# A hybrid decoder step: RMS norms by chunk made from 128x3 values, x turned where it is used, w_ada split in two

## The chip, the cores and the metric

The kernel runs on one core of one Trainium2 chip. The core has a matrix engine (PE, which loads stationary weights with LDWEIGHTS, in the profile PEld, and streams a moving operand past them into PSUM), VectorE (DVE), ScalarE (ACT), GpSimd (POOL) and SyncE (SP, which here only starts DMAs). The metric is device time in microseconds for one launch; lower is better.

## The reference, cut to what matters

One layer: attention and pooling branches, then two sandwiched residual steps and an MLP, for 1024 prompt tokens and 8 sample tokens. Shift, scale and gate vectors come from a conditioning vector c through `w_ada`.

```python
def rms_norm(x, g):
    y = x32 * lax.rsqrt(jnp.mean(x32 * x32, axis=-1, keepdims=True) + EPS)
    return (y * g.astype(jnp.float32)).astype(x.dtype)
def adaln(c, w_ada, b_ada):                    # w_ada is 1024 x 6144
    m = jnp.einsum('nd,de->ne', jax.nn.silu(c), w_ada) + b_ada
    ...
    m = jnp.einsum('ntd,de->nte', m, w_o)
    x = x + gate1 * rms_norm(m, g_post_mix)
    h = rms_norm(x, g_pre_mlp) * (1.0 + scale2) + shift2
    f = einsum(square(relu(einsum(h, w_ff1))), w_ff2)
    x = x + gate2 * rms_norm(f, g_post_mlp)
```

## The kernel before

All activations lie feature by token: a tile is [128 features, KD = 8 feature blocks, T = 1032 tokens]. Products are made in fp32r, a fast form of fp32 with fewer bits: each operand is split into a high part (ACT copies it, `hi`) and a rest (POOL or DVE subtracts, `lo`), and hi·hi + hi·lo + lo·hi are added in PSUM. Semaphores order everything; every engine runs its own list in order.

**Stage A (rest of the projection into the layer, with the last two thirds of w_ada).** Fifteen units u: `g.multiply` (72 products 344 wide), then on PE `turn_ada(u-1)` and `condition(u)`. `condition` multiplies 256 columns of `w_ada` with the 9 conditioning columns `cT`, in plain fp32, straight from the DMA's buffer `wa` (two slots). ACT and POOL only split the projection's weights (`cut_hi`, `cut_lo`), in a loop. A sixteenth `condition` follows the last unit.

**Stage B (chunks).** The tokens are cut into three chunks of 384, 384 and 264 (256 prompt, 8 sample). PE runs 24 products with w_o (`wo(n)`, n = 0..23, eight output blocks for each chunk, each 24 matmuls) and then 12 with the first blocks of w_ff1 (`up_chunk(n)`, n = 24..35), through four PSUM banks. For each chunk there are two norms: of w_o's result (`sum_mo`, then `make_x1` adds it to x) and of the new x (`sum_x1`, then `make_h2`). ACT squares, POOL adds the squares up over the eight feature blocks, PE multiplies the 128x384 sums with a matrix of ones, so that every partition holds every token's sum, and `stats` makes 1/rms on DVE over 128x384 values. POOL multiplies half of the blocks with it (`scale`). x comes in token by feature early, is turned by PE (`turn_x`) between `wo(2)` and `wo(7)` and copied to `xT` by DVE (`take_x`).

**Stage C (main MLP).** 52 weight tiles of 72 products, one after the other. **Stage D (end).** The last w_ff2 products chunk by chunk (`end(n)`, 24 of them), the third norm for each chunk (`sum_y`, `make_y`), the result turned back (`turn_y`) and written out.

## Time and profile before

| | us |
|---|---|
| timed runs | 2067.61, 2073.70, 2076.02 (median 2073.70) |
| the profiled execution | 2078.76, with a span of 2077.0 from first to last instruction |
| stage A, 71 to 309 | 238 |
| attention and pooling, 309 to 1128 | 819 |
| stage B, 1128 to 1362 | 234 |
| stage C, 1362 to 1956 | 594 |
| stage D, 1956 to 2077 | 121 |

The profiled execution is one run with the hardware profiler on; its own time lies 5.06 us above the median of the timed ones. A table by stage shows the share of each stretch in which an engine had work, and the granted clock of PE in that stretch (1.00 is 2.4 GHz, 0.50 is 1.2 GHz).

### The profile page before, as it was taken

The numbers are of one execution on the slowest core, as the hardware profiler recorded it, in microseconds if no ns is written. First come the engines' busy times: TensorE is split into PE (matmuls) and PEld (weight loads), VectorE is DVE, ScalarE is ACT, GpSimd is POOL, SyncE is SP. The second block draws the span as 40 slices with busy tenths as digits, with TensorE's granted clock in tenths as the row PEclk, the third lists the DMA queues.
The fourth block names the chain that finished last, engine by engine and source line by source line (L and its number), as shares of the span: only waits on it lengthen the run. The fifth ranks groups of instructions, "written<-read, shape, count | busy, mean of one in ns | idle before, by whom it ended". The sixth has DMA issues, their size and how long they took to land. (4 is left out here: it accounts for less than half of the span.)

```text
span 2077.0 us, 26057 instructions
## 1 busy us (share of the span) xinstructions
PE 1806.8 (87%) x10834; PEld 1640.5 (79%) x10834; DVE 759.6 (37%) x1381; ACT 555.9 (27%) x1042; POOL 606.7 (29%) x457
## 2 busy tenths in 40 slices
PE   6899995678889888896799786599999999999996
PEld 2788874467777776774699776599999999999996
DVE  2311114244456555663334468721121112111246
ACT  3200001024445544552224123321022012102312
POOL 1211101014445543441024147322112111211332
PEclk9899997988989998998699998799999999999998
DMA  8343325301110100002254002121111111111412
GB/s 265 82 119 95 98 66 162 88 24 42 45 35 28 35 24 21 21 28 79 84 168 137 32 31 71 32 61 41 51 46 47 48 45 51 42 51 41 132 47 67
DMA packets 210486, 139.24 MB, mean 67 GB/s; under 512 B 53317, under 2 KB 206065, under 8 KB 210329
## 3 DMA queue, kind: packets, MB, share of 16 engines
q1 hardware_dynamic: 195611, 124.14, 20.9%
q10 hardware_dynamic: 14758, 13.44, 2.0%
q8 instruction: 86, 1.41, 0.3%
q14 instruction: 31, 0.25, 0.0%
HBM read 117.95 MB, written 21.92 MB: 67 GB/s over the span
## 5 line engine op out<-in xcount | busy, mean ns | idle before, releaser
L1257 POOL TENSOR_SCALAR prob<-prob,share 128x16 f32<-128x16 f32 (+8 forms) x180 | 198.7, 1122 | 290.0 <-DVE share L1296 290.0
L1971 POOL TENSOR_TENSOR ff_lo<-ff_raw,ff_hi 128x1024 fp32r<-128x1024 f32 x56 | 137.0, 2449 | 481.3 <-ACT ff_hi L1792 481.3
L1087 PE MATMUL gate_ps<-h_hi,gate_w_hi 128*128 128x344 f32 x384 | 144.6, 377 | 17.7 <-ACT gate_sum L1214 10.6
L172 POOL TENSOR_TENSOR w_lo<-w_raw,w_hi 128x512 fp32r<-128x512 f32 (+1 forms) x31 | 55.7, 1801 | 331.3 <-ACT w_hi L168 241.2
L2110 PE MATMUL ff_acc<-h_hi,ff_hi 128*128 128x344 f32 x672 | 142.7, 321 | 0.6 <-DVE relu_c L2257 0.6
L2110 PE MATMUL ff_acc<-h_lo,ff_hi 128*128 128x344 f32 x672 | 142.7, 321 | 0.0
L2110 PE MATMUL ff_acc<-h_hi,ff_lo 128*128 128x344 f32 x672 | 141.9, 320 | 0.0
L1306 DVE TENSOR_TENSOR p_lo<-pT,p_hi 128x512 fp32r<-128x512 f32 (+1 forms) x148 | 101.8, 688 | 106.9 <-ACT p_hi L1196 106.3
L1185 ACT ACTIVATE prob<-scores,bias 128x640 f32<-128x640 f32 (+7 forms) x192 | 105.8, 556 | 96.8 <-DVE bias L1282 58.0
L1196 ACT ACTIVATE p_hi<-pT 128x512 fp32r<-128x512 f32 (+1 forms) x148 | 88.2, 596 | 159.2 <-PE pT L1141 158.4
L1087 PE MATMUL gate_ps<-h_lo,gate_w_hi 128*128 128x344 f32 x384 | 128.6, 335 | 0.0
L1087 PE MATMUL gate_ps<-h_hi,gate_w_lo 128*128 128x344 f32 x384 | 128.5, 335 | 0.0
L1141 PE MATMUL pT<-ident,prob 128*128 128x128 f32 (+1 forms) x592 | 96.9, 289 | 34.1 <-POOL prob L1257 34.1
L2110 PE MATMUL ff_acc<-f_hi,ff_hi 128*128 128x344 f32 x576 | 122.5, 321 | 1.8 <-issue 1.8
L2110 PE MATMUL ff_acc<-f_lo,ff_hi 128*128 128x344 f32 x576 | 122.3, 321 | 0.0
L2110 PE MATMUL ff_acc<-f_hi,ff_lo 128*128 128x344 f32 x576 | 121.7, 320 | 0.0
L1792 ACT ACTIVATE ff_hi<-ff_raw 128x1024 fp32r<-128x1024 f32 x56 | 58.7, 1051 | 217.8 <-DMA ff_raw<-in_w_ff_dram 217.8
L2110 PEld LDWEIGHTS ff_acc<-h_lo,ff_hi 128*128 128x128 f32 x672 | 113.8, 189 | 0.0
L2110 PEld LDWEIGHTS ff_acc<-h_hi,ff_hi 128*128 128x128 f32 x672 | 113.1, 188 | 0.8 <-issue 0.8
L2110 PEld LDWEIGHTS ff_acc<-h_hi,ff_lo 128*128 128x128 f32 x672 | 112.0, 188 | 0.0
L1141 PEld LDWEIGHTS pT<-ident,prob 128*128 128x128 f32 (+1 forms) x592 | 69.3, 142 | 52.7 <-POOL prob L1257 37.3
L2339 DVE TENSOR_SCALAR relu<-ff_acc 128x1032 f32<-128x1032 f32 x28 | 34.5, 1233 | 200.1 <-PE ff_acc L2110 200.1
(368 smaller groups left out, 4087.1 us busy)
## 6 DMA issues: line engine op xcount, KB each, us to landing
ff_raw<-in_w_ff_dram SPq DMA_DIRECT2D x56, 512.0 KB, 4.0
wa_rest<-in_w_ada_dram SPq DMA_DIRECT2D x16, 1024.0 KB, 5.3
gate_spill<-gate_sum SPq DMA_DIRECT2D x48, 172.0 KB, 1.9
gates<-gate_spill SPq DMA_DIRECT2D x16, 516.0 KB, 4.8
wa<-in_w_ada_dram SPq DMA_DIRECT2D x8, 1024.0 KB, 9.8
gate_w_raw<-in_w_in_dram SPq DMA_DIRECT2D x16, 512.0 KB, 4.1
w_raw<-in_w_in_dram SPq DMA_DIRECT2D x30, 256.0 KB, 6.3
xt<-in_x_prompt_dram ACTq DMA_DIRECT2D x4, 1024.0 KB, 9.3
```

The costliest lines, as they stand in the source:

```text
L172: pool.tensor_tensor(self.w.lo[:, s, 0:k], self.w.raw[:, s, 0:k], self.w.hi[:, s, 0:k].bitcast(F32), ALU.subtract).then_inc(self.lo_ready, 1)
L1087: last = pe.matmul(gps[:, 0:CH], a[:, u % 2, k], h[:, k, c * CH:(c + 1) * CH], start=(k == 0 and n == 0), stop=(k == KD - 1 and n == 2))
L1141: last = pe.transpose(pT[t % RING][0:m, g * P:(g + 1) * P], prob[:, g, c:c + m], ident[:])
L1185: last = act.activation(prob[:, k, to:to + m], ps[:, c0:c0 + m], ACT.Exp, scale=SCALE, bias=bias[:, par, k, which:which + 1], accum_out=to ...
L1196: act.activation(p_hi[0:m, t % RING], pT[t % RING][0:m, :], ACT.Copy).then_inc(phi_ready, 1)
L1257: last = pool.tensor_scalar(y, y, share[:, n // 2 % 2, g, which:which + 1], None, ALU.mult)
L1306: dve.tensor_tensor(p_lo[0:m, t % RING], pT[t % RING][0:m, :], p_hi[0:m, t % RING].bitcast(F32), ALU.subtract)\
L1792: act.activation(hi, raw, ACT.Copy).then_inc(wfhi_ready, 1)
L1971: pool.tensor_tensor(lo, raw, hi.bitcast(F32), ALU.subtract).then_inc(wflo_ready, 1)
L2110: last = pe.matmul(accs[s][:, c, 0:CH], w[:, z % SLOTS, k], x[:, k, c * CH:(c + 1) * CH], start=(k == 0 and n == 0), stop=(k == KD - 1 and ...
L2339: dve.tensor_scalar(by_chunk(relu[:]), out(m % 2), 0.0, None, ALU.max).then_inc(ff_taken[m % 2], 1)
```

## The change

**w_ada.** `wa` is split like every other weight: ACT copies it to `wa_hi` (one buffer), POOL subtracts into `wa_lo` (in the place of `wa`). c is split too (`c_st`, 9 high and 9 rest columns). `condition` is now two fp32r products for each feature block, 18 and 9 columns wide; the two halves of the 18 rows are added when the rows are turned (a product with `fold`). The ACT and POOL loops are written out, a `cut_ada` after every `cut`.

**Norms.** `add_up` makes the sum for each token with the squares as the stationary operand and one column of ones: 128x1 for each block of 128 tokens, 128x3 in all. `stats` works on 128x3. `spread_out` multiplies 1/rms, broadcast along the free axis, with the identity, and so spreads it over all partitions in PSUM, where DVE reads it. `norm_bank` has two banks. POOL's `scale` and `end_scale` are gone: DVE multiplies all blocks. In `make_h2` DVE only multiplies; the scale and shift is an activation on ACT (`h2_shift`).

**x.** The three x blocks of a chunk are loaded later, into parts of `xT` that are free by then. PE turns them two feature blocks at a time between or in the middle (`halfway`) of products, and `make_x1` reads the turned block from PSUM. The copies to `xT` are gone; `turn_x` waits for `x1_ready`, since there are two PSUM tiles for it.

The norms at the end (`sum_y`, `stats`, `make_y`) are changed in the same way, and `turn_y` pairs are moved one or two products earlier in the list.

```diff
             def condition(pe, c):
-                pe.wait_ge(wa_loaded[c % 2], 16 * (c // 2 + 1))
+                pe.wait_ge(walo_ready, c + 1)
                 if c:
                     pe.wait_ge(arow_ready, c)
+                else:
+                    pe.wait_ge(cst_ready, 1)
                 for k in range(KD):
-                    last = pe.matmul(adaP[:], cT[:, k], wa[:, c % 2, k], start=(k == 0), stop=(k == KD - 1))
+                    pe.matmul(adaP[:], c_st[:, k], wa_hi[:, k], start=(k == 0), stop=False, skip_group_check=True)
+                    last = pe.matmul(adaP[0:1 + NS], c_st[:, k, 0:1 + NS], wa_lo[:, c % 2, k], start=False, stop=(k == KD - 1),
+                                     skip_group_check=True)
                 last.then_inc(ada_done, 1)
...
-                    last = pe.transpose(adaT[:, n], arow[:, c % 2, n * P:(n + 1) * P], ident[0:1 + NS, 0:1 + NS])
+                    last = pe.matmul(adaT[:, n], arow[:, c % 2, n * P:(n + 1) * P], fold[:], start=True, stop=True)
...
+            def cut_ada_hi(act, c):
+                act.wait_ge(wa_loaded[c % 2], 16 * (c // 2 + 1))
+                if c:
+                    act.wait_ge(ada_done, c)
+                act.activation(wa_hi[:], wa[:, c % 2], ACT.Copy).then_inc(wahi_ready, 1)
+            def cut_ada_lo(pool, c):
+                pool.wait_ge(wahi_ready, c + 1)
+                pool.tensor_tensor(wa_lo[:, c % 2], wa[:, c % 2], wa_hi[:].bitcast(F32), ALU.subtract).then_inc(walo_ready, 1)
...
                 def _(act):
-                    with act.Fori(1, NU // 2) as j:
-                        g.cut_hi(act, j, 0)
-                        g.cut_hi(act, j, 1)
-                    g.cut_hi(act, NU // 2, 0)
+                    act.activation(c_st[:, :, 0:1 + NS], cT[:], ACT.Copy).then_inc(chi_ready, 1)
+                    cut_ada_hi(act, 0)
+                    for u in range(NU):
+                        if u + 2 < NU:
+                            g.cut_hi(act, u // 2 + 1, u % 2)
...
+        def x_block(c, b, k):
+            if c == 2:
+                return xlast[:, b, k]
+            if c == 1 and b == 2:
+                return xthird[:, k]
+            at_column = CUT[c + 1][0] + b * P
+            return xT[:, k, at_column:at_column + P]
...
+                    def load_x(dst, b, c):
+                        sp.dma_start(dst, xb[:, b]).then_inc(x_loaded[c], 16)
+                    sp.wait_ge(mlo_ready[1], KD)
+                    for b in range(3):
+                        load_x(xT[:, :, CUT[1][0] + b * P:CUT[1][0] + (b + 1) * P], b, 0)
+                    sp.wait_ge(mlo_ready[2], KD)
+                    for b in range(2):
+                        load_x(xT[:, :, CUT[2][0] + b * P:CUT[2][0] + (b + 1) * P], 3 + b, 1)
...
+                    sp.wait_ge(x1_ready, 2 * KD)
+                    for b in range(2):
+                        load_x(xlast[:, b], 6 + b, 2)
+                    sp.dma_start(xlast[0:NS, 2], x_sample[:, 0, :].rearrange("n (k j) -> n k j", k=KD)).then_inc(x_loaded[2], 16)
                     spill(1)
...
+                    def h2_shift(c, k):
+                        t = h2[:, k, CUT[c][0]:CUT[c][0] + PROMPT[c]]
+                        act.wait_ge(h2t_ready, c * KD + k + 1)
+                        act.activation(t, t, ACT.Identity, scale=sc2[:, k, 0:1], bias=ada[:, 3 * KD + k, 0:1]).then_inc(h2_ready, 1)
                     def h2_cut(c, k0, k1):
+                        h2_shift(c, k0)
                         for k in range(k0, k1):
+                            if k + 1 < k1:
+                                h2_shift(c, k + 1)
                             act.wait_ge(h2_ready, c * KD + k + 1)
...
-                    def scale(c):
-                        pool.wait_ge(rstd_ready, 2 * c + 1)
-                        for k in range(1, KD, 2):
-                            pool.tensor_tensor(part(term[:, k], c), mo[c][:, k, 0:WIDTH[c]], rstd[:, 0:WIDTH[c]], ALU.mult)\
-                                .then_inc(scaled, 1)
...
+                    def turn_x(c, k0, k1):
+                        for k in range(k0, k1):
+                            e = c * KD + k
+                            if k == 0:
+                                pe.wait_ge(x_loaded[c], 48)
+                            if e >= 2:
+                                pe.wait_ge(x1_ready, e - 1)
+                            for b in range(3):
+                                m = NS if c == 2 and b == 2 else P
+                                last = pe.transpose(tp[e % 2][:, b * P:b * P + m], x_block(c, b, k)[0:m], ident[0:m, 0:m])
+                            last.then_inc(xT_done, 1)
...
+                    def add_up(count, c, squares):
+                        for b, m in tokens_of(c):
+                            last = pe.matmul(norm_bank[count % 2][0:m, CW + b:CW + b + 1], squares[:, b * P:b * P + m], ones[:, 0:1],
+                                             start=True, stop=True)
+                        last.then_inc(summed, 1)
+                    def spread_out(count, c, r):
+                        pe.wait_ge(rs_ready, count)
+                        for b, m in tokens_of(c):
+                            last = pe.matmul(norm_bank[count % 2][:, b * P:b * P + m], r[0:m, b:b + 1].broadcast_to([m, P]), ident[0:m, 0:m],
+                                             start=True, stop=True)
+                        last.then_inc(spread, 1)
...
                     def sum_mo(c):
                         pe.wait_ge(sq_added, (KD - 1) * (c + 1))
                         if c:
-                            pe.wait_ge(mean_ready, 2 * c)
-                        pe.matmul(nps[:, 0:WIDTH[c]], ones[:], sqsum[:, 0:WIDTH[c]], start=True, stop=True).then_inc(summed, 1)
+                            pe.wait_ge(x1_ready, KD * c)
+                        add_up(2 * c + 1, c, sqsum)
...
+                    def halfway(c, k0, k1):
+                        return lambda k: turn_x(c, k0, k1) if k == KD // 2 else None
...
                     for n in range(KD):
                         wo(n, before=(lambda k: pe.wait_ge(mlo_ready[0], k + 1)) if n == 0 else None)
-                        if n >= 2:
-                            for e in range(4 * (n - 2), 4 * (n - 1)):
-                                turn_x(e)
                     wo(8)
-                    pe.wait_ge(x_loaded[3], 16)
-                    pe.wait_ge(xT_taken, 3 * KD - 1)
-                    for k in range(KD):
-                        last = pe.transpose(tp[0][:, k * NS:(k + 1) * NS], xblk2[0:NS, 0, k * P:(k + 1) * P], ident[0:NS, 0:NS])
-                    last.then_inc(xT_done, 1)
                     sum_mo(0)
-                    for n in range(9, 13):
-                        wo(n)
+                    wo(9)
+                    spread_out(1, 0, rs)
+                    turn_x(0, 0, 2)
+                    wo(10, halfway(0, 2, 4))
+                    turn_x(0, 4, 6)
+                    wo(11, halfway(0, 6, 8))
+                    wo(12)
+                    wo(13)
                     sum_x1(0)
-                    for n in range(13, 17):
-                        wo(n)
...
+                    def stats(count, r, v, t):
                         dve.wait_ge(summed, count)
-                        dve.tensor_scalar(v[:, 0:w], nps[:, 0:w], 1.0 / D, EPS, ALU.mult, ALU.add).then_inc(mean_ready, 1)
+                        dve.tensor_scalar(v[:], norm_bank[count % 2][:, CW:CW + 3], 1.0 / D, EPS, ALU.mult, ALU.add).then_inc(mean_ready, 1)
                         dve.wait_ge(root_ready, count)
-                        chain.then_wait(dve.reciprocal(r[:, 0:w], r[:, 0:w]))
-                        chain.then_wait(dve.scalar_tensor_tensor(t[:, 0:w], r[:, 0:w], -0.5, r[:, 0:w], ALU.mult, ALU.mult))
-                        chain.then_wait(dve.tensor_tensor(t[:, 0:w], t[:, 0:w], v[:, 0:w], ALU.mult))
-                        dve.scalar_tensor_tensor(r[:, 0:w], t[:, 0:w], 1.5, r[:, 0:w], ALU.add, ALU.mult).then_inc(rstd_ready, 1)
-                        dve.wait_ge(rstd_ready, count)
-                    def residual(x, t, gate, c):
+                        chain.then_wait(dve.reciprocal(r[:], r[:]))
+                        chain.then_wait(dve.scalar_tensor_tensor(t[:], r[:], -0.5, r[:], ALU.mult, ALU.mult))
+                        chain.then_wait(dve.tensor_tensor(t[:], t[:], v[:], ALU.mult))
+                        dve.scalar_tensor_tensor(r[:], t[:], 1.5, r[:], ALU.add, ALU.mult).then_inc(rs_ready, 1)
...
                     def make_x1(c, k0, k1):
+                        w = WIDTH[c]
+                        dve.wait_ge(spread, 2 * c + 1)
                         for k in range(k0, k1):
+                            e = c * KD + k
                             t = part(term[:, k], c)
-                            if k % 2:
-                                dve.wait_ge(scaled, 4 * c + k // 2 + 1)
-                            else:
-                                chain.then_wait(dve.tensor_tensor(t, mo[c][:, k, 0:WIDTH[c]], rstd[:, 0:WIDTH[c]], ALU.mult))
-                            residual(part(xT[:, k], c), t, gt1[:, k], c).then_inc(x1_ready, 1)
+                            chain.then_wait(dve.tensor_tensor(t, mo[c][:, k, 0:w], norm_bank[1][:, 0:w], ALU.mult))
+                            dve.wait_ge(xT_done, e + 1)
+                            residual(part(xT[:, k], c), t, gt1[:, k], tp[e % 2], c).then_inc(x1_ready, 1)
...
                     def make_h2(c, k0, k1):
                         p, w = PROMPT[c], WIDTH[c]
+                        dve.wait_ge(spread, 2 * c + 2)
                         for k in range(k0, k1):
                             t = part(h2[:, k], c)
-                            chain.then_wait(dve.tensor_tensor(t, part(xT[:, k], c), rstd[:, 0:w], ALU.mult))
                             if p < w:
+                                chain.then_wait(dve.tensor_tensor(t[:, p:w], xT[:, k, TP:T], norm_bank[0][:, p:w], ALU.mult))
                                 chain.then_wait(dve.tensor_tensor(t[:, p:w], t[:, p:w], sc2[:, k, 1:], ALU.mult))
                                 dve.tensor_tensor(t[:, p:w], t[:, p:w], ada[:, 3 * KD + k, 1:], ALU.add)
-                            dve.tensor_scalar(t[:, 0:p], t[:, 0:p], sc2[:, k, 0:1], ada[:, 3 * KD + k, 0:1], ALU.mult, ALU.add)\
-                               .then_inc(h2_ready, 1)
+                            dve.tensor_tensor(t[:, 0:p], xT[:, k, CUT[c][0]:CUT[c][0] + p], norm_bank[0][:, 0:p], ALU.mult).then_inc(h2t_ready, 1)
...```

What stands on DVE from the last `wo` copy before the first norm to the first x1 blocks, before (`rstd`, `mean` and `ntmp` are the norm's 128x384 tiles, `term` the scaled result of w_o):

```order
L2201 COPY mo_10169<-ff_acc 128x384
L2280 COPY xT<-x_tp 128x8x8
L2212 TENSOR_SCALAR mean<-ff_acc 128x384
L2214 RECIPROCAL rstd<-rstd 128x384
L2215 SCALAR_TENSOR_TENSOR ntmp<-rstd 128x384
L2216 TENSOR_TENSOR ntmp<-ntmp,mean 128x384
L2217 SCALAR_TENSOR_TENSOR rstd<-ntmp,rstd 128x384
L2201 COPY mo_10169<-ff_acc 128x384 x2
L2235 TENSOR_TENSOR term<-mo_10166,rstd 128x384
L2226 SCALAR_TENSOR_TENSOR xT<-term,gt_60,xT 128x384 x2
```

The same place on DVE after (`mv`, `rs`, `nt` are the 128x3 tiles, `ff_acc` in the products is 1/rms in PSUM):

```order
L2310 COPY mo_10405<-ff_acc 128x384
L2315 TENSOR_SCALAR mv<-ff_acc 128x3
L2317 RECIPROCAL rs<-rs 128x3
L2318 SCALAR_TENSOR_TENSOR nt<-rs 128x3
L2319 TENSOR_TENSOR nt<-nt,mv 128x3
L2320 SCALAR_TENSOR_TENSOR rs<-nt,rs 128x3
L2310 COPY mo_10405<-ff_acc 128x384
L2337 TENSOR_TENSOR term<-mo_10402,ff_acc 128x384
L2328 SCALAR_TENSOR_TENSOR xT<-term,gt_60,x_tp 128x384
```

The five steps of the norm are three values wide, one copy stands between them and the first x1 block instead of two, and x is read from `x_tp`.

On POOL from the adds of w_o's first chunk to those of the second, before (`sqsum` takes the squares of w_o's result, `h` those of x1, `h_lo` is the rest of h2):

```order
L1937 TENSOR_TENSOR sqsum<-sqsum,sq 128x384 x7
L1949 TENSOR_TENSOR term<-mo_10166,rstd 128x384 x4
L1937 TENSOR_TENSOR sqsum<-sqsum,sq 128x384 x3
L1958 TENSOR_TENSOR h_10158<-h_10158 128x384 x7
L1937 TENSOR_TENSOR sqsum<-sqsum,sq 128x384 x4
L1964 TENSOR_TENSOR h_lo<-h_10158,h_hi 128x384 x8
L1949 TENSOR_TENSOR term<-mo_10169,rstd 128x384 x4
```

The same on POOL after:

```order
L2007 TENSOR_TENSOR sqsum<-sqsum,sq 128x384 x8
L2021 TENSOR_TENSOR h_10394<-h_10394 128x384 x3
L2007 TENSOR_TENSOR sqsum<-sqsum,sq 128x384
L2021 TENSOR_TENSOR h_10394<-h_10394 128x384 x4
L2007 TENSOR_TENSOR sqsum<-sqsum,sq 128x384 x3
L2027 TENSOR_TENSOR h_lo<-h_10394,h_hi 128x384 x4
L2007 TENSOR_TENSOR sqsum<-sqsum,sq 128x384
L2027 TENSOR_TENSOR h_lo<-h_10394,h_hi 128x384 x4
L2007 TENSOR_TENSOR sqsum<-sqsum,sq 128x384
```

The products with 1/rms are gone, and the last two adds of the second chunk's squares (n = 14 and 15), which stood ahead of all `h_lo` of the first chunk, now stand between and behind them.

## Rows read from the trace of the kernel before

**Rows 1.** The page's first part: engines' busy time, share of span, instructions.

```profile
PE 1806.8 (87%) x10834; PEld 1640.5 (79%) x10834; DVE 759.6 (37%) x1381; ACT 555.9 (27%) x1042; POOL 606.7 (29%) x457
```

**Rows 2.** Busy time by stage: stretch, length, engines, PE clock, DMA share, GB/s.

```profile
71.00:309.00 238.00, 235.91 (x1368) 197.43 (x1368) 27.34 (x54) 13.73 (x13) 30.46 (x14) 0.99 0.38 100
1128.00:1362.00 234.00, 170.88 (x949) 164.01 (x950) 155.73 (x241) 68.20 (x135) 106.88 (x89) 0.85 0.17 55
1362.00:1956.00 594.00, 592.16 (x3748) 591.62 (x3749) 98.41 (x81) 110.19 (x108) 128.52 (x53) 1.00 0.16 46
```

**Rows 3.** Timeline of one unit of stage A: start, length, engine, work, [wait].

```profile
161.59 1.06 ACT L168 ACTIVATE w_hi<-w_raw 128x1024 fp32r<-128x1024 f32 x1 [14.32 <-PE in_acc L202]
161.64 3.62 PE L516 MATMUL ada_rest<-wa_rest,cT 128*9 128x256 f32 x16
162.73 2.34 POOL L172 TENSOR_TENSOR w_lo<-w_raw,w_hi 128x1024 fp32r<-128x1024 f32 x1 [13.04 <-ACT w_hi L168]
165.19 0.74 PE L202 MATMUL in_acc<-h_hi,w_hi 128*128 128x344 f32 x3
...
176.96 3.41 PE L516 MATMUL ada_rest<-wa_rest,cT 128*9 128x256 f32 x15
```

**Rows 4.** Timeline of PE, the end of stage A.

```profile
299.52 3.62 PE L516 MATMUL ada_rest<-wa_rest,cT 128*9 128x256 f32 x16
...
303.87 3.62 PE L516 MATMUL ada_rest<-wa_rest,cT 128*9 128x256 f32 x16
```

**Rows 5.** Timeline of PE in stage B: turning x, and waits.

```profile
1147.40 1.33 PE L2031 MATMUL x_tp<-ident,x_three 128*128 128x128 f32 x6 [4.56 <-DVE xT L2207]
...
1179.75 0.82 PE L2031 MATMUL x_tp<-ident,x_three 128*128 128x128 f32 x6
...
1221.27 1.65 PE L2067 MATMUL ff_acc<-h,ones 128*128 128x384 f32 x2 [9.49 <-POOL h L1958]
...
1346.68 0.59 PE L2018 MATMUL ff_acc<-h_hi,wo_hi 128*128 128x264 f32 x1 [7.69 <-POOL h_lo L1964]
```

**Rows 6.** The chain that ended last, PE's pieces: start, us, what.

```profile
1128.02 9.97 PE ff_acc L2018 x48
...
1189.31 4.21 PE ff_acc L2018 x24
...
1346.68 14.60 PE ff_acc L2018 x96
...
2027.49 2.90 PE ff_acc L2018 x24
```

**Rows 7.** Timeline of DVE in stage B: a reciprocal, and h2.

```profile
1197.44 2.55 DVE L2214 RECIPROCAL rstd<-rstd 128x384 f32<-128x384 f32 x1 [1.90 <-ACT rstd L1771]
...
1238.67 1.37 DVE L2243 TENSOR_TENSOR h<-xT,rstd 128x384 f32<-128x384 f32 x1
```

**Rows 8.** Two lines on DVE: count, ns min/median/max, first and last start, forms.

```profile
L2226 DVE SCALAR_TENSOR_TENSOR xT<-term,gt,xT x24: 473/798/1368, 1205.3 to 1320.8; 128x384 f32<-128x384 f32 x16, 128x256 f32<-128x256 f32 x8
...
L2364 DVE TENSOR_TENSOR fT<-ff_acc,fT x24: 415/558/559, 1961.2 to 2053.7; 128x384 f32<-128x384 f32 x16, 128x264 f32<-128x264 f32 x8
```

**Rows 9.** Timelines of ACT and POOL, runs of operations without a wait between.

```profile
1126.76 3.42 ACT L1751 ACTIVATE m_hi<-mT 128x384 fp32r<-128x384 f32 x8 [9.03 <-PEq L1525]
...
1201.85 4.26 POOL L1949 TENSOR_TENSOR term<-mo,rstd 128x384 f32<-128x384 f32 x4 [12.91 <-DVE rstd L2217]
```

**Rows 10.** Groups by line and form on DVE: count, busy us, mean ns.

```profile
L2207 DVE COPY xT<-x_tp 128x384 f32<-128x384 f32 x16 | 8.2, 551 | 0.9 <-PE x_tp L2031 0.9
L1295 DVE RECIPROCAL share<-share 128x4 f32<-128x4 f32 x32 | 5.7, 179 | 1.1
```

**Rows 11.** The chain in stage D: sum of the last chunk, and its first product.

```profile
2055.48 0.73 PE ff_acc L2147 x2
...
2060.39 0.44 DVE yterm L2375
```

**Rows 12.** Timeline of PE in stage D: turning the second chunk's result.

```profile
2050.11 0.66 PE L2158 MATMUL x_tp<-ident,yterm 128*128 128x128 f32 x4 [1.24 <-DVE yterm L2226]
```

More of the change, by code:

```diff
@@ new lines, in _ @@
+                    cut_wo_hi(act, 4)
+                    for k in range(4):
+                        m_cut(1, k)
+                    cut_wo_hi(act, 5)
+                    for k in range(4, KD):
+                        m_cut(1, k)
+                    square(0)
+                    cut_wo_hi(act, 6)
+                    for k in range(4):
+                        m_cut(2, k)
+                    square(1)
+                    cut_wo_hi(act, 7)
+                    for k in range(4, KD):
+                        m_cut(2, k)
@@ L1825, in _ @@
+                    for n in range(2, 9):
+                        square(n)
+                    root(1)
                     square(9)
+                    x1_squares(0, 0, 4)
                     square(10)
-                    x1_squares(0, 0, 4)
+                    x1_squares(0, 4, 8)
                     square(11)
-                    x1_squares(0, 4, 8)
                     square(12)
+                    root(2)
                     square(13)
-                    root(2, 0)
+                    h2_cut(0, 0, 4)
@@ L2053, in up_chunk, with tokens_of @@
                         _, hi, lo = weights(t)
-                        product(bank[n % 4], hi, lo, h2_hi, h2_lo, c).then_inc(prod_done, 1)
+                        product(bank[n % 4], hi, lo, h2_hi, h2_lo, c, before).then_inc(prod_done, 1)
+                    def tokens_of(c):
+                        return [(b, NS if c == 2 and b == 2 else P) for b in range(3)]
+                    def add_up(count, c, squares):
[9 more added lines that the diff above has]
+                        last.then_inc(spread, 1)
                     def sum_mo(c):
@@ L2089, in _ @@
+                    spread_out(3, 1, rs)
+                    turn_x(1, 0, 2)
+                    wo(18)
+                    turn_x(1, 2, 4)
+                    wo(19)
+                    turn_x(1, 4, 6)
+                    wo(20)
+                    turn_x(1, 6, 8)
+                    wo(21)
+                    wo(22)
                     sum_x1(1)
-                    for n in range(22, 24):
-                        wo(n)
+                    wo(23)
+                    spread_out(4, 1, rs)
@@ L2092, in _ @@
                     up_chunk(24)
                     sum_mo(2)
-                    for n in range(25, 29):
-                        up_chunk(n)
+                    up_chunk(25)
+                    spread_out(5, 2, rs)
+                    turn_x(2, 0, 2)
+                    up_chunk(26, halfway(2, 2, 4))
+                    turn_x(2, 4, 6)
+                    up_chunk(27, halfway(2, 6, 8))
+                    up_chunk(28)
                     sum_x1(2)
-                    for n in range(29, 36):
+                    up_chunk(29)
@@ L2098, in _ @@
+                    spread_out(6, 2, rs)
+                    for n in range(30, 36):
                         up_chunk(n)
@@ L2280, in _ @@
-                    dve.tensor_copy(xT[:, :, TP:T], tp[0][:, 0:KD * NS].rearrange("p (k n) -> p k n", k=KD)).then_inc(xT_taken, 1)
-                    stats(1, WIDTH[0], rstd, mean, ntmp)
+                    for k in range(4):
+                        m_rest(1, k)
+                    collect(0)
+                    for k in range(4, KD):
+                        m_rest(1, k)
+                    collect(1)
+                    for k in range(4):
+                        m_rest(2, k)
+                    collect(2)
```

302 lines of the change are left out of this document (148 added, 154 removed).

## The prediction

> **What bounds the kernel now.** I read the page's first part, then a table by stage, then timelines of the stages that the change touches, then the chain. PE is busy 1806.8 us, 87% of the span [rows 1]: this is a kernel of matrix products, and a change is worth what it takes off PE's work or off PE's waits. The table by stage [rows 2] says which of the two, where. Stage A: PE busy 235.9 of 238 us at clock 0.99, so only less work on PE helps. Stage B: 170.9 of 234 at clock 0.85; 63 us are waits, and part of the busy time is slow. Stage C: 592.2 of 594 at 1.00, and the change doesn't touch it. So I build stages A, B and D from their rows, against the profiled execution (2078.76 us, span 2077.0), which is 5.06 above the median of 2073.70.
>
> **Stage A, w_ada.** A condition holds PE from 161.64 to 165.19, 3.55 us; the next starts at 176.96, so a unit takes 15.32 and 11.77 lie between conditions [rows 3]. After, it is 16 fp32r products 256 wide. Nearest row: 24 fp32r products 264 wide in 2.90 [rows 6], 0.121 each, so 0.117 at 256 and 1.88 for 16; the fold costs 0.14 more (one transpose more at 0.82/6 [rows 5]). Saved: 3.55 - 2.02 = 1.53, in 15 units 23.0.
> That row is 0.117 for a product. The Trainium skill ("TensorE: Matmul & The Clock Gate", section "Back-to-back issue gap") gives 262 cycles at a moving size of 256; by it 16 products would take about 1.75 (an estimate), and the units 2 us more would be saved. I go by the row.
> Cover: wa has to be cut first, and `wa_hi` is one buffer, so the cut starts when the last condition ends. ACT 128x2048 costs twice 1.06, POOL twice 2.34 [rows 3], with hand-offs 0.2: 2.1 + 4.7 + 0.2 = 7.0, against 11.8 of the multiply: hidden, 4.8 to spare. Behind these two steps `cut_hi` and `cut_lo` for two units on are queued; they have a unit's time. The load of wa into the freed slot has a whole period. If this cover failed, the units would be longer by what is missing, bounded by the gain (0).
> The sixteenth condition has no multiply ahead: PE starts it at 303.87, 0.7 after the end of the one at 299.52 [rows 4]. After, it waits for the 7.0: +6.3, less a gain of 0.6 (its own products are shorter, but come after a wait): +5.7. Stage A: -23.0 + 5.7 = **-17.3**, bounds -23 and 0.
>
> **Stage B, PE's work.** It lasts from 1128.02 to stage C's first tile at 1361.9, 233.9 us. Its products in full flow: 4.21 for 384 columns, 2.90 for 264 [rows 6], so 24 x 4.21 + 12 x 2.90 = 135.8. The first two take 9.97, not 8.42 [rows 6]: +1.55. Turning x: 64 transposes at 0.137 [rows 5] and 8 small ones, 9.4. Norms: six sums and six spreads of three small products; none is in the trace. The nearest row is 0.73 for two records of a sum [rows 11], the bounds are 0.5 (three transposes, with the wait for the weights) and 1.3 (under the 1.65 at [rows 5]); I take 0.75, 9.0 in all, bounds 6 to 15.6. Together 155.8.
>
> **What goes.** Turning waits for DVE's copies 16 times, 4.56 us the first time [rows 5]; the copies (16 of 0.551 and the smaller ones [rows 10]) go, and x is turned after the sum, when the bank is free. The 384-wide reciprocal of 2.55 [rows 7] becomes a step on 128x3, nearest row 0.179 on 128x4 [rows 10]; so does each other step. The norm's chain after the sum is then five such steps, a root and a spread, 1.5 to 3 us, and lies under `wo(9)` (4.2) or `up_chunk`s (2.9). POOL's products, four at 4.26 us a chunk [rows 9], go. `make_x1`'s sum takes 0.473 to 1.368 with both operands in SBUF, while a DVE operation that reads PSUM never exceeds 0.559 [rows 8]: two engines that read SBUF seem to get into each other's way (inferred; the spread is the fact), and the new operands are in PSUM. So the 9.49 wait before the first chunk's second sum [rows 5] should go, and `wo(0)` to `wo(8)` run without a gap.
> The Trainium skill ("VectorE: DVE Perf Modes", "Rules for kernel authors") advises to copy from PSUM to SBUF first where many operations read it. By that rule 24 copies more, about 13 us of DVE, would pay for themselves; by [rows 8] an operation from PSUM costs 0.56 at 384 columns, as much as a copy, so I don't count them.
>
> **What is late next.** Three waits of PE remain or are new.
> (1) `sum_mo(1)`. From the second spread PE has `wo(15)` and `wo(16)`, 7.1 us. In the new order POOL does eight `h_lo` and two adds first, 10 x 1.07 (4.26/4 [rows 9]) = 10.7, and starts 1.8 later (one DVE product, two ACT steps of 0.5). 12.5 - 7.1: 5.4, less 0.2 for what else PE does there: 5.2.
> (2) Chunk 2's turns. Two tiles hold the turned x, so each pair of turns waits until DVE has done with the pair before. A block there is two operations of 0.42 [rows 8] and two on 8 columns of 0.18 [rows 10], 1.2, a pair 2.4, and DVE takes a product's result between pairs, 0.55; PE has half of an `up_chunk` of chunk 0 and a pair of turns beside it, 2.1 + 0.27. Lost: 0.5 three times, 1.5. In chunk 0 a pair takes 2 x 1.07 (0.56 and 0.5) and every second one 0.55 more: about covered; in chunk 1 whole products stand between.
> (3) `up_chunk(32)`. From the last spread PE has 8.4 (two `up_chunk`s and turning's rest). DVE makes eight blocks of h2 at 1.2 (one 0.42 product, three 8-column ones at 0.18 and 0.2 for their hand-offs; bounds 0.9 and 1.5), 9.6, and the relu of `up_chunk(30)`, which stands behind them in DVE's list, 0.5; behind that wait on ACT `hidden_chunk(30)` and the cuts of h2, eight at 0.43 (3.42/8 [rows 9]) with the 264-wide less, 4.1 with the first's hand-off, then POOL 0.8: 15.0. The wait is 6.6, much like today's 7.69 there [rows 5].
> Together 13.3, between 0 and 25. After a wait PE is slow: the last four products take 14.60 instead of 11.60 after 7.69 of waiting [rows 5, 6], 3.0; I count it for (3) and two thirds of it for (1): 5. x itself is not late, I expect: chunk 0's loads start when the low part of the second chunk's input is made, some six products (25 us) before the turns; the last chunk's stand behind four loads of weights in SP's list and have, by my estimate, 5 us to spare, the smallest margin; if that is gone, PE waits there for what is missing.
> Stage B: 155.8 + 13.3 + 5 = 174.1, so **-59.8**; bounds -78 (none of the waits) and -40 (15.6 for the norms and nearly twice the waits).
>
> **Stage D.** From the end of the last sum (2055.48 + 0.73) to the first product with 1/rms (2060.39) are 4.2 us [rows 11]; after, five steps of 0.18, a root, hand-offs and a spread, 2.2: -2.0. Two earlier spreads cost 1.4 (two of 0.7), and PE's wait for `make_y(1)`, 1.24 [rows 12], goes, since the turns move behind another product. Behind the sum DVE takes POOL's four products, 4 x 0.46 (0.415 to 0.558 [rows 8]) = 1.9; POOL no longer runs beside it, for which I take back 1.3, one and a half times the 0.9 between a delayed operation and a free one (1.368 - 0.473 [rows 8]). Together **-1.2**, bounds -4 and +3. Stage C: 0.
>
> **Sum.** -17.3 - 59.8 - 1.2 = -78.3. The profiled execution goes from 2078.8 to 2000.5, the median from 2073.7 to **1995**.
>
> **Rivals.**
> (a) The waits don't come: POOL and ACT are ahead, DVE's operations take 0.47, as the fastest do [rows 8]. Then 13.3 + 5 go too: 1977. For: [rows 8] shows the fast case. Against: (1) and (3) are sums of many operations, in an order that is fixed.
> (b) DVE sets stage B: its x1 and h2 operations keep the longest time that they show today, 1.37 [rows 7, 8]. A pair in chunk 0 is then 2 x (0.56 + 1.37) = 3.9 against 2.4, 1.5 lost three times, 4.5, and 1.0 for the result taken between; in chunk 2, with 0.91 at 256 columns, 3.4 and 0.3 against 2.4, 1.3 three times, 3.9, of which 1.5 is counted; h2 in (3) is later by 8 x 0.5 = 4; and PE is slow after each of six more waits by some 0.8 (5 us for the two large ones above), 5. Together 4.5 + 1.0 + 2.4 + 4 + 5 = 17, 2012. For: DVE now does all that POOL did. Against: those that took so long had POOL beside them and read SBUF alone.
> (c) The cut of w_ada is not hidden, or its products are no faster: stage A gains nothing, 2013. For: one buffer, so ACT, POOL and PE go in turn. Against: 4.8 us to spare.
> (d) Slower than before. PE is at clock 0.85 in stage B and 1.00 in stage C [rows 2]; if the turns, spreads and waits in the middle of products keep it at 1.2 GHz there, 135.8 us of products take twice that: 1995 + 136 = 2131. It decides from 78.3/135.8, 58% of them at the lower level. Against: today's stage has longer waits and products still take 4.21 [rows 6].
> (e) The change does not do what it says: stage A gains nothing, as in (c), and in stage B each wait that goes comes back as another, so that PE waits the 63 us of today and its products are slow behind them as today. Only stage D's 1.2 stay: 2072.5. Against: the longest of today's waits hang on operations that are no longer there.
>
> **How the numbers follow.** Forecast 0.48 (its own range 1985 to 2006), (a) 0.17, (b) 0.20, (c) 0.10, (d) 0.03, (e) 0.02. The range must reach into (a), to 1972, since the norms may cost 3 us less too and stage A may reach its -23; upwards past (b) and (c), to 2020. A measurement of this kernel can tell about 0.5% (10 us) from no change: all of the forecast, (a), (b) and (c) are faster by more, 0.95; (e) is the same, 0.02; (d) is slower, 0.03.
>
> **What would show it.** Right: in stage A conditions of 1.9 us in periods of 13.8, no wait for POOL in the units, one of 7 before the last condition. In stage B `wo(0)` to `wo(8)` without a gap; waits of about 5 before `sum_mo(1)` and 6.6 before `up_chunk(32)`; the two DVE lines of x1 near 0.56 with none at 1.37; spreads of 0.75. Stage C as long as before at 1.00. Wrong: periods near 15.3; PE waiting for DVE before turns (b); a clock in stage B under 0.85 (d); a last-chunk wait for x's load, which I took to have a margin of 5.

## The result

The changed kernel took 2004.0 us (median of 2003.52, 2003.8, 2004.2 and 2008.4), the kernel before, timed beside it, 2074.86: a ratio of 0.9668 with a 95% interval of 0.9638 to 0.9697. The forecast was 1995, with a range of 1972 to 2020. The profiled execution took 2003.8 us, with a span of 2002.0.

The page's first part and its row of TensorE's clock, after:

```profile
PE 1776.5 (89%) x10956; PEld 1641.2 (82%) x10956; DVE 692.9 (35%) x1366; ACT 595.6 (30%) x1083; POOL 648.1 (32%) x449
...
PEclk9899987879989998999689999999999999999998
```

[rows 1] had PE at 1806.8. So TensorE's work fell by 30 us, while the time fell by 71: more than half of the gain is waiting that is gone. The table by stage says where, as in [rows 2] (stretch, length, busy time of PE, PEld, DVE, ACT and POOL, PE clock, DMA share, GB/s). The cuts are now at PE's own instructions: first condition, start of the last product of the last one, first `wo` product, first tile of the main MLP, first product of the end. After:

```profile
84.40:290.10 205.70, 199.68 (x1325) 189.75 (x1323) 26.26 (x49) 42.59 (x28) 100.01 (x28) 0.98 0.40 103
290.10:1106.44 816.34, 656.57 (x3903) 561.33 (x3901) 393.14 (x864) 308.00 (x697) 274.64 (x227) 0.89 0.21 62
1106.44:1282.26 175.82, 162.62 (x1008) 159.19 (x1009) 97.32 (x212) 77.46 (x159) 86.65 (x77) 0.94 0.24 73
1282.26:1879.91 597.65, 591.94 (x3744) 591.14 (x3745) 98.07 (x80) 110.33 (x108) 128.60 (x53) 1.00 0.16 46
1879.91:2002.00 122.09, 107.24 (x686) 104.10 (x684) 47.30 (x107) 28.47 (x51) 34.00 (x27) 0.92 0.31 92
```

The same cuts before gave 222.10, 820.92, 233.87, 593.48 and 121.63. Set against the forecast:

| stretch | before | after | change | forecast |
|---|---|---|---|---|
| stage A, w_ada | 222.1 | 205.7 | -16.4 | -17.3 |
| attention, pooling | 820.9 | 816.3 | -4.6 | 0 |
| stage B, chunks | 233.9 | 175.8 | -58.1 | -59.8 |
| stage C, main MLP | 593.5 | 597.7 | +4.2 | 0 |
| stage D, end | 121.6 | 122.1 | +0.5 | -1.2 |

In stage B PE waits 175.8 - 162.6 = 13.2 us; it waited 63.1. The list of PE's waits there (who waited, for whom: us in total, times, the longest), after:

```profile
PE ff_acc L2078 <- POOL h_lo L2027: 6.0, 1, 6.0
PE ff_acc L2124 <- POOL sqsum L2007: 5.1, 1, 5.1
PE ff_acc L2078 <- DVE m_lo L2303: 4.3, 1, 4.3
PE ff_acc L2132 <- DVE rs L2320: 1.5, 2, 1.0
PE ff_acc L2211 <- DVE relu_c L2360: 0.6, 1, 0.6
```

The 4.3 lie ahead of the stage's first product, as before. The same list of the kernel before began with what has gone:

```profile
PE ff_acc L2067 <- POOL h L1958: 34.3, 3, 12.8
PE x_tp L2031 <- DVE xT L2207: 12.4, 6, 4.6
PE ff_acc L2018 <- POOL h_lo L1964: 11.1, 2, 7.7
```

The 34.3 were three waits for the second norm of each chunk (POOL's adds, behind x1, behind POOL's own products), the 12.4 those for the copies of x.

### The profile page after: what moved, and what is told of

It is laid out like the page before. It is cut to its first block and busy times, and to the rows that moved or that the text cites. A ratio compares the mean times of both kernels' runs of the same rounds, so it can differ in the third digit from the quotient of the medians.

```text
span 2002.0 us, 26313 instructions
## 1 busy us (share of the span) xinstructions
PE 1776.5 (89%) x10956; PEld 1641.2 (82%) x10956; DVE 692.9 (35%) x1366; ACT 595.6 (30%) x1083; POOL 648.1 (32%) x449
## 5 line engine op out<-in xcount | busy, mean ns | idle before, releaser
L1119 PE MATMUL gate_ps<-h_hi,gate_w_hi 128*128 128x344 f32 x384 | 143.0, 372 | 18.3 <-ACT gate_sum L1246 11.1
L2211 PE MATMUL ff_acc<-h_hi,ff_hi 128*128 128x344 f32 x672 | 142.7, 321 | 0.6 <-DVE relu_c L2360 0.6
L2211 PE MATMUL ff_acc<-h_lo,ff_hi 128*128 128x344 f32 x672 | 142.6, 321 | 0.0
L2211 PE MATMUL ff_acc<-h_hi,ff_lo 128*128 128x344 f32 x672 | 141.9, 320 | 0.0
L172 POOL TENSOR_TENSOR w_lo<-w_raw,w_hi 128x512 fp32r<-128x512 f32 (+1 forms) x31 | 56.4, 1821 | 233.7 <-ACT w_hi L168 143.5
L2211 PE MATMUL ff_acc<-f_lo,ff_hi 128*128 128x344 f32 x576 | 122.3, 321 | 3.7 <-issue 3.7
L2211 PE MATMUL ff_acc<-f_hi,ff_hi 128*128 128x344 f32 x576 | 122.4, 321 | 2.0 <-issue 2.0
L2211 PE MATMUL ff_acc<-f_hi,ff_lo 128*128 128x344 f32 x576 | 121.7, 320 | 0.0
L2211 PEld LDWEIGHTS ff_acc<-h_lo,ff_hi 128*128 128x128 f32 x672 | 113.8, 189 | 0.0
L2211 PEld LDWEIGHTS ff_acc<-h_hi,ff_hi 128*128 128x128 f32 x672 | 113.1, 188 | 0.8 <-issue 0.8
L2211 PEld LDWEIGHTS ff_acc<-h_hi,ff_lo 128*128 128x128 f32 x672 | 112.0, 188 | 0.0
L1865 ACT ACTIVATE fraw<-relu 128x1032 f32<-128x1032 f32 x28 | 29.9, 1067 | 266.0 <-DVE relu L2443 266.0
```

Of the source, the lines that this page charges most:

```text
L172: pool.tensor_tensor(self.w.lo[:, s, 0:k], self.w.raw[:, s, 0:k], self.w.hi[:, s, 0:k].bitcast(F32), ALU.subtract).then_inc(self.lo_ready, 1)
L1119: last = pe.matmul(gps[:, 0:CH], a[:, u % 2, k], h[:, k, c * CH:(c + 1) * CH], start=(k == 0 and n == 0), stop=(k == KD - 1 and n == 2))
L1865: act.activation(fraw[:, t], relu[:], ACT.Square).then_inc(f_squared, 1)
L2211: last = pe.matmul(accs[s][:, c, 0:CH], w[:, z % SLOTS, k], x[:, k, c * CH:(c + 1) * CH], start=(k == 0 and n == 0), stop=(k == KD - 1 and ...
```

## Experiments

Each is the changed kernel with the edit shown, unless it says otherwise. Stage lengths are of the profiled execution, cut as above. The attention stretch took between 810 and 822 us in these profiles, though nothing there was touched; so edits are judged by their stage, and totals by several runs. e1, e5 to e8 and e11 are one execution each. Where an edit doesn't touch the chunks, they took 175.9 (e2), 175.4 (e8) and 174.0 (e7).

**The kernel before, again (e1).** No edit.

> The kernel before, unchanged, profiled a second time. The first profile of it was 5 us above the median, and its stretch from the end of the last w_ada product to the first w_o product (attention and pooling, which the change doesn't touch) was 820.5 us, against 816.0 in the changed kernel. If that difference is only the spread from one execution to the next, this profile shows 814 to 818 there and a total of 2070 to 2075. If the change really shortened that stretch, it shows 820 to 821 again. In both cases the w_o chunks (first w_o product to the first tile of the main MLP) take 233 to 235, and the main MLP 598 to 599.

Total 2074.2; attention 816.7, chunks 233.7, main MLP 594.1. So the 4.6 us of the table's second line are no effect of the change, and what is to be explained is 2074.9 to 2004.0.

**w_ada undone (e2).**

```diff
-pe.matmul(adaP[:], c_st[:, k], wa_hi[:, k], ...)
-last = pe.matmul(adaP[0:1 + NS], c_st[:, k, 0:1 + NS], wa_lo[:, c % 2, k], ...)
+last = pe.matmul(adaP[:], cT[:, k], wa[:, c % 2, k], ...)
```

> The changed kernel with the w_ada part undone (plain fp32 products, as before). Theory: the three parts are separate, so only the projection's units get longer again, by 16.4 us: periods of 15.3 instead of 13.8, no wait before the last one; total 2004 + 16 = 2020. Rival: what w_ada gave is taken back behind it (the next stage waits for a transfer anyway): total within 4 us of 2004. In the main MLP the two pairs of waits without a releaser stay where they are if they depend on how many instructions of TensorE stand ahead of its loop modulo 256, since 256 fewer stand there.

2016.4 (2013.56 to 2018.3); stage A 222.1, chunks 175.9 as with it. The part is worth its 16.4 us and nothing of it is taken back. The total rose by 4 less than that because the main MLP took 593.5 instead of 597.7: the expectation that its second waits would stay was wrong (below).

**1/rms in SBUF (e3).**

```diff
+if k0 == 0:
+    chain.then_wait(dve.tensor_copy(nrm[:, 0:w], norm_bank[1][:, 0:w]))
...
-chain.then_wait(dve.tensor_tensor(t, mo[c][:, k, 0:w], norm_bank[1][:, 0:w], ALU.mult))
+chain.then_wait(dve.tensor_tensor(t, mo[c][:, k, 0:w], nrm[:, 0:w], ALU.mult))
```

(and so in `make_h2`.)

> The changed kernel, but the spread 1/rms is copied from PSUM to SBUF once for each of the six norms of the chunks (the three at the end are left), and the products of x1 and h2 read it there: two operands in SBUF instead of one. Theory (an operand in PSUM keeps VectorE from being held up by GpSimd): beside GpSimd the products go from 0.55 us to 1.0 to 1.4, six copies add 0.5 each, and the chunks take 8 to 15 us longer: 2012 to 2019. Rival (where the operand lies makes no difference, a copy and two reads are as good): the products stay at 0.47 to 0.56, and the total is 2004 to 2006.

2017.2 (2013.83 to 2023.26); chunks 187.5, 11.6 more. Groups of one line on DVE (ns of the shortest, median and longest operation, first and last start), h2's product, first of the changed kernel:

```profile
L2351 DVE TENSOR_TENSOR h<-xT,ff_acc x24: 406/546/555, 1177.9 to 1260.7; 128x384 f32<-128x384 f32 x16, 128x256 f32<-128x256 f32 x8
```

and with the operand in SBUF:

```profile
L2355 DVE TENSOR_TENSOR h<-xT,nrm x24: 412/550/2769, 1182.3 to 1276.1; 128x384 f32<-128x384 f32 x16, 128x256 f32<-128x256 f32 x8
```

The median is the same; the longest goes from 0.56 to 2.77 us, and the 24 take 20.3 us instead of 10.9 (x1's products 16.4 instead of 12.1). The second chunk's eight, in the changed kernel's timeline of DVE,

```profile
1219.23 3.80 DVE L2351 TENSOR_TENSOR h<-xT,ff_acc 128x384 f32<-128x384 f32 x8 [0.68 <-PE ff_acc L2132]
```

and in this run's chain:

```profile
1225.63 11.50 DVE h L2355 x8
```

The next norm's steps stand behind them in DVE's list. TensorE sees it in its waits, of this run: 6.7 for `rs` instead of 1.5.

```profile
PE ff_acc L2133 <- DVE rs L2321: 6.7, 2, 5.6
```

So leaving 1/rms in PSUM is worth 11.6 us here, the six copies of this run (3.0 us of VectorE) included. The Trainium skill ("SBUF — State Buffer", section "Who interferes with whom") says that a VectorE instruction with two inputs in SBUF contends with a GpSimd one that reads SBUF, and one with at most one such input, outside its two-port modes, doesn't; the two groups agree, 0.56 against 2.77 at most.

**Norms over 128x384 (e4).** The sum again by a matrix of ones to all partitions, `stats` over w columns in SBUF, no spread:

```diff
-dve.tensor_scalar(v[:], norm_bank[count % 2][:, CW:CW + 3], 1.0 / D, EPS, ALU.mult, ALU.add)
+dve.tensor_scalar(v[:, 0:w], norm_bank[count % 2][:, 0:w], 1.0 / D, EPS, ALU.mult, ALU.add)
...
-chain.then_wait(dve.reciprocal(r[:], r[:]))
+chain.then_wait(dve.reciprocal(r[:, 0:w], r[:, 0:w]))
```

> The changed kernel with the norms undone: TensorE's sum against a matrix of ones puts every token's sum on all partitions, and root, reciprocal and the three steps after it run over 128x384 in SBUF, all nine norms; VectorE still does all products, and x is still turned just in time and read from PSUM. Theory: x's part and the norms' part each gave about half; the chunks get 20 to 30 us longer than in the changed kernel (8 to 15 by the operand in SBUF, as in e3, the rest by chains of 5 us instead of 1.5 to 3 that products no longer cover): 2024 to 2034. Rival (the 128x3 values themselves give nothing, since the longer chain also lies under products): the same as e3, within 3 us.

2024.05 (2021.33 to 2025.94); chunks 191.1, the end 126.2 instead of 122.1. In the chunks the norms' part is worth 15.3: 11.6 as in e3, and 3.7 that this run adds. The 3.7 are the width, less what this run does without: e3's six copies, and six spreads of 0.67 to 1.02 us on TensorE. The theory gave the width more (it expected 20 to 30 in the chunks); the rival, within 3 us of e3, nearly held there. At the end, where nothing covers the last norm, undoing it costs 4.1.

**x copied first (e10).**

```diff
-residual(part(xT[:, k], c), t, gt1[:, k], tp[e % 2], c).then_inc(x1_ready, 1)
+xs = part(xT[:, k], c)
+chain.then_wait(dve.tensor_copy(xs, tp[e % 2][:, 0:w]))
+residual(xs, t, gt1[:, k], xs, c).then_inc(x1_ready, 1)
```

> The changed kernel, but each turned block of x is first copied from PSUM to SBUF by VectorE (24 copies of 0.42 to 0.55 us), and the sum of x1 reads it there, so that this operation too has two operands in SBUF. Theory: 24 copies cost 12 us of VectorE, of which TensorE sees what its turns wait for (a pair of blocks 3.4 to 3.6 against 2.4 of products in the first and last chunk), and the sums that run beside GpSimd go to 0.9 to 1.3: chunks 183 to 190, total 2011 to 2018. Rival (copying first costs nothing that shows): chunks 175 to 178, total 2004 to 2006.

2014.15 (2010.17 to 2015.76); chunks 186.7, 10.9 more. Turns now wait for DVE, which the changed kernel's list doesn't have; the second line is the group of the sum of x1:

```profile
PE x_tp L2092 <- DVE xT L2328: 7.5, 9, 1.4
```

```profile
L2328 DVE SCALAR_TENSOR_TENSOR xT<-term,gt,xT x24: 472/624/1207, 1154.9 to 1255.4; 128x384 f32<-128x384 f32 x16, 128x256 f32<-128x256 f32 x8
```

The longest sum is 1.21, where it was 0.617 from PSUM, and the 24 take 17.5 us instead of 13.6. The copies themselves take 12.4, so this run shows the price of copying more than that of the operand's place. The Trainium skill ("VectorE: DVE Perf Modes", section "Rules for kernel authors") says to read PSUM as it is, or to copy to SBUF first where many operations follow. The prediction took x for such a case, but one operation reads each block of x. The case here is 1/rms, which eight products read, and copying it first, in e3, cost 11.6 us: there the measurement decides against the copy.

**Both (e11).** e4 and e10 together.

> e4 and e10 together: norms over 128x384 in SBUF and x copied from PSUM first; x is still turned just in time, VectorE still does all products and ScalarE h2's scale and shift. What is then left of the difference to the kernel before (233.9 in the chunks) is worth what turning later, and the other division of work between GpSimd, VectorE and ScalarE, give. Theory: the two costs add up, as VectorE is what the turns wait for: chunks 200 to 208. Rival: they hide in each other: 191 to 196.

Chunks 201.3; one execution, 2034.7. The costs add up: 175.8 + 15.3 + 10.9 = 202.0. So the 58.1 us of stage B fall into three: 32.6 (233.9 to 201.3) for turning x later and for the new division of work between GpSimd, VectorE and ScalarE, 10.2 for reading x from PSUM without a copy, 15.3 for the norms. The 32.6 were not split further.

**The order of GpSimd's list (e5).** The wait of 5.1 before `sum_mo(1)`. In the changed kernel's timeline of POOL (start, length, work, [wait]) the adds of products 14 and 15 stand between and behind the `h_lo`, as the order said:

```profile
1180.26 4.03 POOL L2027 TENSOR_TENSOR h_lo<-h,h_hi 128x384 fp32r<-128x384 f32 x4 [5.48 <-ACT h_hi L1841]
1184.24 1.01 POOL L2007 TENSOR_TENSOR sqsum<-sqsum,sq 128x384 f32<-128x384 f32 x1
1185.21 3.86 POOL L2027 TENSOR_TENSOR h_lo<-h,h_hi 128x384 fp32r<-128x384 f32 x4
1189.02 1.00 POOL L2007 TENSOR_TENSOR sqsum<-sqsum,sq 128x384 f32<-128x384 f32 x1
```

```diff
-adds(11, 14)
-h2_rest(0, 0, 4)
-adds(14, 15)
-h2_rest(0, 4, 8)
-adds(15, 18)
+adds(11, 15)
+h2_rest(0, 0, 3)
+adds(15, 16)
+h2_rest(0, 3, 8)
+adds(16, 18)
```

(ScalarE's squares 14 and 15 move up to match.)

> The changed kernel with two lines of GpSimd's list and two of ScalarE's in another order: the squares and adds of products 14 and 15 come ahead of most cuts of h2's first chunk, so that sum_mo(1) no longer stands behind eight h_lo. Theory: TensorE's 5.1 us before sum_mo(1) go, and the sum itself is shorter (0.6 instead of 1.4 after a wait); the h_lo that are later now have 30 us until up_chunk(24). Chunks 169 to 171 instead of 175.9. Rival: the wait moves on to the next thing that needs GpSimd (the second norm of that chunk): 174 to 176.

No wait before `sum_mo(1)`; chunks 167.1, 8.7 less. More than expected, but 2.5 of it is chance: this execution's first nine products took 39.4 instead of 40.85, its last four 13.4 instead of 14.5, at a higher granted clock (0.96 for 0.93, and 0.88 for 0.81). e7, whose edit doesn't touch the chunks, shows the same 39.4 and 13.3. Some 6.3 belong to the edit.

**Sample columns at once (e6).**

```diff
+ts = h2[:, :, TP:T]
+chain.then_wait(dve.tensor_tensor(ts, xT[:, :, TP:T], norm_bank[0][:, p:w].unsqueeze(1).broadcast_to([P, KD, NS]), ALU.mult))
+... two more, in place of three for each block
```

> The changed kernel with h2's sample columns of the last chunk made for all eight blocks in three operations of 128x8x8 instead of 24 of 128x8. Theory: VectorE's eight blocks before relu(30) shrink from 8.2 us to about 4, and the 6.0 us wait of TensorE before up_chunk(32) falls to 1 to 3, with less slow product behind it: chunks 170 to 173. Rival: ScalarE (two operations a block) and GpSimd set the pace there anyway: wait 5 to 6, chunks 175 to 176.

The wait before `up_chunk(32)` fell from 6.0 to 2.3, the four products behind it from 14.5 to 11.9; chunks 169.6, 6.2 less. So the 24 small operations set most of that wait. It cost more than itself: the granted clock from its end to the end of the stage was 0.81 in the changed kernel and is 1.00 here, so 3.7 us less of waiting gave 6.2.

PE's wait, and the chain's piece behind it:

```profile
PE ff_acc L2078 <- POOL h_lo L2027: 2.3, 1, 2.3
```

```profile
1268.18 11.88 PE ff_acc L2078 x96
```

**The last condition (e7).** A second `wa_hi` over the raw weights, for the sixteenth alone:

```diff
+wa_hi2 = buf.slabs(5)("wa_rest_hi2", [P, KD, AC], F32R)
+high = lambda c: wa_hi2 if c == NU else wa_hi
...
-                if c:
+                if c == NU:
+                    act.wait_ge(g.lo_ready, NU)
+                elif c:
                     act.wait_ge(ada_done, c)
```

> The changed kernel with a second buffer for the high part of w_ada's last columns (over the raw weights, which are free by then), so that ScalarE and GpSimd cut them under the last multiply. Theory: the 5.5 us wait before the last condition goes: stage A 200 instead of 205.7. Rival: the load of these columns, which starts only when the condition two back is done, takes the place of the wait: 203 to 206.

Stage A 198.8, 6.9 less; the wait is gone and so is the lower clock in the condition behind it (2.0 us at a granted clock of 1.00, instead of 3.25 at 0.59).

**Twenty tiny products (e8).** They do no part of the computation and stand where TensorE waits for a transfer.

```diff
 turn_ada(pe, NU)
+for _ in range(20):
+    pe.matmul(adaP[0:1 + NS, 0:1], cT[:, 0], ones[:, 0:1], start=True, stop=True)
```

> The changed kernel with 20 tiny products (9x1) more on TensorE at the end of the w_ada stage, where it waits for a transfer anyway. They compute nothing that is used; they only move all later TensorE instructions by a few dozen places. Theory: in the main MLP's loop the second wait without a releaser (1.6 and 2.1 us, 12 products after each jump back) comes from loading of code in pieces, with the loop's start shortly ahead of a piece's end; moved past it, only the first wait of each pair (0.9 and 1.1) is left: main MLP 593.5 to 594 instead of 597.6. Rival: the second waits come from something else (data, clock): 597 to 598 with the gaps still after 12 products.

The chain in the main MLP (start, us, what; "issue" is time in which PE waited for nothing that the profile shows) of the changed kernel,

```profile
1509.82 0.89 issue
1510.71 2.16 PE ff_acc L2211 x12
1512.87 1.58 issue
1514.45 180.11 PE ff_acc L2211 x1140
1694.56 1.11 issue
1695.67 2.15 PE ff_acc L2211 x12
1697.82 2.12 issue
```

and with the 20 products:

```profile
1515.74 0.85 issue
1516.59 182.12 PE ff_acc L2213 x1152
1698.71 0.82 issue
```

The second wait is gone at both jumps back, and the stage takes 593.3. The total of this one execution, 2005.0, says nothing: its attention stretch took 821.6.

**All four (e9).** e5 to e8 together.

> The changed kernel with the four edits of e5 to e8 together. Theory: they lie in different places of TensorE's path and add up: stage A 199 (-6.9), chunks 161 (-8.8 and -6.3), main MLP 593.5 (-4.1): total 2004 - 26 = 1978, ratio to the kernel before about 0.954. Rival: the two edits in the chunks share a cause (what one gives the other can't give again), so that the chunks stay at 166 to 168: total 1983 to 1985.

1983.2 (1976.35 to 1987.45, six runs), a ratio to the kernel before of 0.9562 (0.9537 to 0.9586), and 20.8 less than the changed kernel's 2004.0. The total lies where the rival had it, but the chunks' 163.3 lie nearer to the theory's 161 than to the rival's 166 to 168. By stage:

```profile
85.30:284.20 198.90, 198.39 (x1325) 189.04 (x1323) 26.27 (x49) 42.60 (x28) 100.12 (x28) 1.00 0.41 106
...
1101.70:1265.04 163.34, 158.02 (x1008) 154.59 (x1009) 94.54 (x191) 77.37 (x159) 87.52 (x77) 0.98 0.26 78
1265.04:1858.57 593.53, 591.62 (x3744) 591.08 (x3745) 98.07 (x80) 110.32 (x108) 128.64 (x53) 1.00 0.16 46
```

Stage A gave 6.8, the chunks 12.5, the main MLP 4.1: 23.4 of the 26 expected. The chunks' 2.6 that are missing are the chance part of e5, some 2.5: the first nine products took 40.85 again, and the last four 11.9, as in e6 alone.

## Why the prediction came out as it did

**Stage A: right, 0.9 too much.** The condition takes 1.88, as forecast from the fp32r row. In ACT's timeline the cuts repeat every 13.87 us, where [rows 3] had 15.32; 1.45 a unit, not 1.53, because the rest of the unit, with the product with `fold`, is 0.22 longer and not 0.14.

```profile
167.23 1.06 ACT L168 ACTIVATE w_hi<-w_raw 128x1024 fp32r<-128x1024 f32 x1 [9.44 <-PE in_acc L202]
169.74 1.92 ACT L547 ACTIVATE wa_rest_hi<-wa_rest 128x2048 fp32r<-128x2048 f32 x1 [1.45 <-PE ada_rest L529]
181.10 1.06 ACT L168 ACTIVATE w_hi<-w_raw 128x1024 fp32r<-128x1024 f32 x1 [9.44 <-PE in_acc L202]
```

and in POOL's:

```profile
171.74 4.60 POOL L552 TENSOR_TENSOR wa_rest_lo<-wa_rest,wa_rest_hi 128x2048 fp32r<-128x2048 f32 x1 [0.98 <-ACT wa_rest_hi L547]
```

The cut takes 1.92 and 4.60 (forecast 2.1 and 4.7) and ends at 176.34, 5.1 us ahead of the next condition at 181.47 (167.60 + 13.87); 4.8 were forecast. The last one waits 5.52, as PE's timeline has it:

```profile
287.20 0.40 PE L528 MATMUL ada_rest<-wa_rest_hi,c_st 128*18 128x256 f32 x1 [5.52 <-POOL wa_rest_lo L552]
```

From the end of the condition before it (280.30 + 0.28) that makes 6.6 us, where 7.0 were forecast. The products behind the wait take 3.25 us, at a granted clock of 0.59, 0.4 less than before where 0.6 less was forecast. So the miss is mainly the 0.08 a unit, fifteen times.

**Stage B: right, 1.7 too much.** Waits of 13.2 for 13.3, and the two largest at the places named: 5.1 before `sum_mo(1)` (5.2), 6.0 before `up_chunk(32)` (6.6). That the sums agree so well is partly luck: the 1.5 for chunk 2's turns did not come, and 1.5 came at two spreads instead and 0.6 before the main MLP. At these spreads `stats` ran beside POOL. Its last step, over three values with both inputs in SBUF, took 2.30 us once, where it takes 0.16 in three other norms:

```profile
1215.90 2.30 DVE L2320 SCALAR_TENSOR_TENSOR rs<-nt,rs 128x3 f32<-128x3 f32 x1
```

POOL's subtraction beside it began at 1215.82, took 2.37 and ended with it. So even a tiny step is held up, which the chain of 1.5 to 3 us in the prediction has no room for.

PE's work was 162.6, against 155.8 and 5 for the clock; 1.4 of the 1.8 more lie in the first nine products, 40.85 where the sum has 39.4, as e5 and e7 show it. Spreads take 0.67 to 1.02 and sums 0.46 to 1.44, around the 0.75 taken. The prediction speaks of 16 waits for x's copies; the list of before has 6. That number is in no term.

The step by which DVE's operations stay short when they read PSUM was inferred from a spread in [rows 8]; e3 shows it, with products of up to 2.77 us. Rival (b), with operations of 1.37, is what e3 looks like, 2017 for the 2012 that it named. The prediction did not say how the gain divides among the parts; the norms' width, a part of its account, gave 3.7 in the chunks.

**Stage D: 1.7 too much.** From the last sum's start to the first product with 1/rms it went from 4.91 to 3.79, 1.1 less where 2.0 were forecast: the spread takes 1.76 there, at a granted clock of 0.50 behind the wait, and not the 0.67 of the two earlier ones. Ahead of that sum, 0.5 of the 1.24 that PE waited for `make_y(1)` stayed, where all was to go, and the turns that moved earlier put one more group of them, 0.9, ahead of the last product, which the forecast left out. From the first product with 1/rms to the end it took 16.6 as before, where 0.6 more was forecast.

**Stage C: the step that failed.** "Stage C: 0" was wrong by 4.2 us, the largest single miss. It stood on the step that the change doesn't touch this stage. TensorE's products are the same; the second waits behind the loop's jumps are new, and moving the code removes them (e8). No row of before could price it: it shows one wait at each jump (1.01 and 0.83).

The misses are 0.9 + 1.7 + 4.2 + 1.7 = 8.5 us; the forecast of 1995 and these make 2003.5, and the median was 2004.0. The first profile's 5.06 above the median, taken off at the outset, was mostly its attention stretch, 820.9 against 816.7 in e1.

## What to carry to other kernels

Where VectorE and GpSimd work side by side, give each VectorE operation one operand in PSUM if TensorE can leave it there: copying 1/rms to SBUF first cost 11.6 us here, though the median of the products that read it hardly changed, and copying x first 10.9, where the copies were most of it. When a wait goes, sum up the queue of the next engine in its new order: two waits were forecast to within 0.6 us so. One then went when lines of that queue were moved; the other fell from 6.0 to 2.3 when 24 small operations ahead of it became three. Changes that are independent by stage should be judged by stage, since a stretch that no edit touched moved by several us between executions.

## What was not expected of the hardware

After a jump back of TensorE's loop there is a wait of 0.8 to 1.4 us in every trace here, and in some a second, 1.4 to 2.4 us, always 12 products on. The second shows in all six kernels with the changed kernel's count of TensorE instructions (10956 products on the page: the changed one, e3, e5, e6, e7, e10) and in none of the others (before 10834, e2 10924, e4 and e11 10866, e8 and e9 10996). The queue that carries instructions moved 89 packets of 16 KB in the former, 86 or 87 in the latter. e8 adds 20 products far ahead of the loop and changes nothing else, so the place of the loop in the code decides; that code is loaded in pieces, with the loop's start just ahead of a piece's end in the changed kernel, fits all of them and is inferred. In e2 the waits were expected to stay, since the edit was thought to remove whole pieces; it removed 32 products.
